# Two transformer blocks, fp32 products in three passes: another way to form the low part of the weights of the last product

## The reference, cut to what matters

```python
D_MODEL, SEQ, D_FF = 1024, 512, 2816

def second_block(x, ..., w_gate, w_up, w_down, final_norm_g):
    ...
    h = rmsnorm_2(x, ffn_norm_g[l])
    x = x + (jax.nn.silu(h @ w_gate[l]) * (h @ w_up[l])) @ w_down[l]
    return rmsnorm_2(x, final_norm_g)
```

## Time and profile before

| what | value |
|---|---|
| median of three timed executions | 1211.48 us |
| lowest and highest of them | 1210.47 and 1211.53 us |
| span of the profiled execution | 1209.1 us |
| TensorE busy, mean granted clock | 98% of the span, 0.998 of full speed |
| ScalarE busy, GpSimd busy | 46%, 41% |
| DMA traffic | 119.71 MB, all of it issued by SP, apart from instruction fetches |

### The profile page before, as it was taken

How to read it: one execution, slowest core, us unless ns; L and a number is a source line. 1 busy time by engine, 2 the same in 40 slices (tenths; PEclk the granted TensorE clock), 3 DMA queues, 4 the chain that set the end, 5 groups by cost and what they waited for, 6 DMA issues and landing times.

```text
span 1209.1 us, 15625 instructions
## 1 busy us (share of the span) xinstructions
PE 1188.8 (98%) x5810; PEld 990.9 (82%) x5810; DVE 629.7 (52%) x1459; ACT 561.4 (46%) x1009; POOL 499.3 (41%) x277
## 2 busy tenths in 40 slices
PE   9999999999999999999999999999999999999997
PEld 8878778888888887799878788788888888888886
DVE  5789864774628264999964773954222231220002
ACT  6453574476522364557765785434322332221114
POOL 1428462345433424123252883444344434443441
PEclk9999999999999999999999999999999999999999
DMA  8204662302332523153123204322332333323211
GB/s 276 81 25 142 173 175 70 105 1 71 122 105 70 186 94 105 35 176 108 36 40 94 81 23 153 103 93 84 105 105 70 105 105 103 102 74 122 104 70 70
DMA packets 80618, 119.71 MB, mean 99 GB/s; under 512 B 16024, under 2 KB 42776, under 8 KB 80160
## 3 DMA queue, kind: packets, MB, share of 16 engines
q1 hardware_dynamic: 80544, 118.71, 30.3%
HBM read 108.20 MB, written 4.21 MB: 93 GB/s over the span
## 4 chain that ended last, share of the span: by engine, by line
PE 80%; DVE 11%; ACT 2%; POOL 2%; issue 2%; DMA 2%; SPq 1%; DVEq 0%; ACTq 0%; POOLq 0%
PE bank L1794 59%; PE bank L2112 9%; PE bank L1858 2%; PE bank L1890 2%; PE bank L1872 2%; PE bank L1936 2%; DVE sc L1472 2%; DVE m L1468 1%; DVE sqS L1618 1%; POOL w_lo L731 1%; PE bank L1834 1%; DMA rot<-in_rot 1%; PE bank L1975 1%; DVE rp L1218 1%; ACT w_hi L834 0%
## 5 line engine op out<-in xcount | busy, mean ns | idle before, releaser
L714 POOL TENSOR_TENSOR w_lo<-w_raw,w_hi 128x2048 fp32r<-128x2048 f32 (+3 forms) x78 | 352.0, 4513 | 584.9 <-ACT w_hi L802 527.6
L1794 PE MATMUL bank<-aH,w_hi 128*128 128x512 f32 x832 | 331.6, 399 | 2.6 <-DVE mqT L1669 1.1
L1794 PE MATMUL bank<-aH,w_lo 128*128 128x512 f32 x832 | 324.9, 391 | 0.0
L1794 PE MATMUL bank<-aL,w_hi 128*128 128x512 f32 x832 | 318.2, 391 | 0.0
L802 ACT ACTIVATE w_hi<-w_raw 128x2048 fp32r<-128x2048 f32 (+3 forms) x74 | 138.4, 1870 | 262.1 <-PE bank L1794 159.5
L1794 PEld LDWEIGHTS bank<-aH,w_hi 128*128 128x128 f32 x832 | 157.0, 189 | 33.5 <-issue 4.7
L1794 PEld LDWEIGHTS bank<-aL,w_hi 128*128 128x128 f32 x832 | 156.3, 188 | 33.4
L1794 PEld LDWEIGHTS bank<-aH,w_lo 128*128 128x128 f32 x832 | 156.9, 189 | 27.8 <-issue 0.2
L1218 DVE TENSOR_TENSOR fg<-bank,rB 128x512 f32<-128x512 f32 x22 | 15.1, 691 | 128.2 <-PE bank L1794 128.2
L1794 PE MATMUL bank<-uH,w_hi 128*128 128x512 f32 x192 | 75.0, 391 | 0.3 <-DVE uL L1690 0.2
L1794 PE MATMUL bank<-uL,w_hi 128*128 128x512 f32 x192 | 74.8, 390 | 0.0
(11 more groups left out here) (337 smaller groups left out, 2124.2 us busy)
## 6 DMA issues: line engine op xcount, KB each, us to landing
w_raw<-in_w_in SPq DMA_DIRECT2D x21, 1024.0 KB, 5.0
w_raw<-in_w_gate SPq DMA_DIRECT2D x22, 512.0 KB, 3.9
w_raw<-in_w_up SPq DMA_DIRECT2D x22, 512.0 KB, 4.8
w_raw<-in_w_down SPq DMA_DIRECT2D x11, 1024.0 KB, 4.8
w_raw<-in_w_merge SPq DMA_DIRECT2D x8, 1024.0 KB, 4.9
w_raw<-in_w_out SPq DMA_DIRECT2D x8, 1024.0 KB, 4.9
w_raw<-in_w_ple_gate SPq DMA_DIRECT2D x4, 1024.0 KB, 4.9
w_raw<-in_w_in SPq DMA_DIRECT2D x4, 512.0 KB, 7.2
```

The costliest lines, as they stand in the source:

```text
L714: pool.tensor_tensor(out=w_lo[:, c % 2, 0:n], in0=w_raw[:, c % 2, 0:n], in1=w_hi[:, c % 2, 0:n].bitcast(F32), op=ALU.subtract).then_inc(w_ ...
L1794: ins = pe.matmul(o, l, r, start=(kk == 0 and operand == ROUNDED and m == 0), stop=(kk == total - 1 and operand == REST), skip_group_check ...
```

## The change

For the chunks of the unit `down`, GpSimd's subtraction is left out. ScalarE, after the hi part, waits for its own result and writes -hi into `w_lo` with a second activation (scale -1.0). GpSimd waits for that and issues a DMA from `w_raw` to `w_lo` in SBUF with `accum_op=add`, so that `w_lo` becomes raw - hi. TensorE, and SP before it reuses the raw buffer, wait for that DMA's semaphore `down_lo`. GpSimd waits before each of these DMAs until the one before has landed. All other chunks are made as before.

```diff
+        turned_ready, down_lo = sem("turned_ready"), sem("down_lo")
...
+        d_first = UNITS["down"][0]
+
+        def lo_wait(eng, c):
+
+            if c < d_first:
+                eng.wait_ge(w_lo_ready, c + 1)
+            else:
+                eng.wait_ge(down_lo, 16 * (c - d_first + 1))
...
                 if c >= 2:
                     sp_.wait_ge(w_hi_ready, c - 1)
-                    sp_.wait_ge(w_lo_ready, c - 1)
+                    lo_wait(sp_, c - 2)
...
             scale_rows("mla", sc2)
-            lo_through(len(CHUNKS) - 1)
+            lo_through(d_first - 1)
+            for c in range(d_first, len(CHUNKS)):
+                n = CHUNKS[c][0] * CHUNKS[c][1]
+                pool.wait_ge(turned_ready, c - d_first + 1)
+                if c > d_first:
+                    pool.wait_ge(down_lo, 16 * (c - d_first))
+                pool.dma_start(w_lo[:, c % 2, 0:n], w_raw[:, c % 2, 0:n], accum_op=ALU.add).then_inc(down_lo, 16)
...
                     act.activation(w_hi[:, c % 2, 0:n], w_raw[:, c % 2, 0:n], ACT.Copy).then_inc(w_hi_ready, 1)
+                    if c >= d_first:
+                        act.wait_ge(w_hi_ready, c + 1)
+                        act.activation(w_lo[:, c % 2, 0:n], w_hi[:, c % 2, 0:n].bitcast(F32), ACT.Copy,
+                                       scale=-1.0).then_inc(turned_ready, 1)
                     nxt[0] = c + 1
...
                 pe.wait_ge(w_hi_ready, c + 1)
-                pe.wait_ge(w_lo_ready, c + 1)
+                lo_wait(pe, c)
                 wh, wl = w_view(w_hi, c), w_view(w_lo, c)
```

## The result

The changed kernel takes 1214.67 us (median of 7 runs) against 1210.47 us of the kernel before on the same chip (7 runs); the ratio is 1.0032, interval 1.0020 to 1.0043. It is slower by 4.2 us by the two medians and by 3.9 us by the ratio; the prediction had 6.5 us, the right way and the right place, and too much.

The account below looks back on a forecast made before the run. TensorE was taken to bound the kernel. The terms 0 (GpSimd) + 0 (ScalarE's queue) + 6.5 us (DMA waits, 5 x 1.3) on 1211.5 us gave 1218.0 us, range 1210.6 to 1235.

Parts of the forecast that it names:

- The bound and the place: Last product: TensorE never waits and sets the pace; taking away GpSimd's subtraction gives nothing.
- Once per pair: Last product: TensorE waits at d2, d4, d6, d8 and d10 only, so each pair of chunks pays once, 5 x s.
- A: Adding DMA's time from GpSimd's release to its last semaphore: taken as 8.0 us, 8.25 with overlap; up to 6.95 fits.
- the longest of the 2 MB rows: Profiled 2 MB transfers took 7.3, 7.8 and 8.0 us; the 8.0 was taken for A as nearest in bytes read.
- My third way: Estimate of the adding DMA: a 1 MB load's 4.8 us plus 3.0 us for a second stream, 7.8 us.
- The budget: Each chunk's hi and lo must be ready 10.88 us after its buffer's release; 3.93 us before the DMA leaves it 6.95.
- The rival "no change": The DMA fits, A up to 7.4 us and loss below 2.4 us, time 1211.5 us; chance 0.3.
- the likeliest case: A between 7.4 and 10 us, losing 2.4 to 15 us, 1214 to 1227 us; chance 0.42.
- ScalarE's queue: Eleven added activations, 21.8 us, mostly in ScalarE's idle time; a Silu starts 0.5 us late; cost on the path 0.
- SP's queue: Loads of chunk c+2 start 5.3 us later but still land before ScalarE wants them, d4's at 1111 against 1117.
- The 0.25 us for the overlap with loads: Added to A where a load's end meets the next adding DMA; estimate 0.25 us, from 0 to 1.

Follow-up runs that it names:

- e2: Kernel before, with GpSimd's subtraction of each chunk of the last product done twice and no DMA of GpSimd's; 1214.42 us, ratio 1.0031.
- e4: Changed kernel with ScalarE's second activation done twice, the second time after a wait for the first; 1223.63 us, ratio 1.0104.
- e5: As e4, but only for d0, d2, d4, d6, d8, d10; the other chunks use GpSimd's subtraction as in the kernel before; 1226.34 us, ratio 1.0128.
- e7: Changed kernel with GpSimd's DMA as a plain copy instead of an addition, hi part's subtraction left out; 1210.19 us, ratio 0.9996.
- e6: Changed kernel with the load of gfin moved from behind the load of d4 to behind that of d10; 1214.46 us, ratio 1.0034.
- e8: Changed kernel with the second activation and the adding DMA each cut in two halves of 128x1024; 1228.06 us, ratio 1.0150.
- e9: As e8, with 1024 instead of 512 bytes per partition set aside for descriptors of GpSimd's DMAs; 1219.83 us, ratio 1.0078.

## Why the prediction came out as it did

**The bound and the place.** Right: TensorE sets the pace, GpSimd's subtraction was worth nothing to it, and the loss lies in the last product alone.

**Once per pair.** Right in kind (e2, e4, e5), not in its detail. I had waits at d2, d4, ... only, with releases 10.9 and 12.2 apart. But the DMAs' landings scatter (6.8 to 7.8 us). d3's took 7.8 us and moved the wait to the odd chunks d3 and d5, d6's took 7.3 and brought it back to the even ones. By the releases the time lost is 0.67 us at d2, 1.0 at d3, nothing at d4, 0.7 and 0.5 at d5 and d6, and 0.2 to 0.5 at each of the others.

**The duration of the DMA.** This is the term that was mis-sized. I took A = 8.25 us from ScalarE's end to the landing; it is 0.35 + 6.9 = 7.25 us. Of the reasons behind 8.25, the longest of the 2 MB rows was no good neighbour: that transfer comes from HBM, and e7 shows that a copy inside SBUF lands 0.3 us sooner than a load. My third way, one MB of load plus 3.0 us for the second stream, had too dear a stream: it costs 2.4 us.
The Trainium skill's page "DMA: Bandwidth & Descriptors" (section "Anatomy of one DMA") came nearest: its fit of 2.0 us plus bytes / 436 GB/s gives, as an estimate, 4.4 us for the copy and 6.8 for two streams; measured are 4.5 and 6.9. The Trainium skill's page "Collectives: The Full Stack" (section "The bandwidth ceiling") says of the adding step of a ReduceScatter that the addition costs nothing and its two reads halve the rate; 6.9 - 4.5 = 2.4 us is what a second MB costs by that fit. The trace agrees in the total, but 0.35 us of the 2.4 lie in GpSimd's longer issue.

**The budget.** The other error went the other way. I let the lo part land 10.88 us after the release; the cycle of a buffer has 0.43 to 0.49 us more in it, from the landing until TensorE runs at its pace. With both terms right, and counted from the hi part's start, it is 3.87 + 0.35 + 6.9 + 10.88 + 0.43 = 22.43 against 21.76, 0.67 us per pair and 3.4 us in all. With the landings that the trace has for each chunk in place of 6.9 (d3's 7.8, d6's 7.3) the same reckoning gives 4.0 us, against the 4.23 us of the trace. The two errors, 1.0 too much and 0.45 too little per pair, left 6.5 us in place of 4.

**The rival "no change".** It was nearer than its 0.3 says. I counted A from ScalarE's end, so the measured A is 7.25 us; by my own sum this costs 5 x 0.3 = 1.5 us, and I had put every A up to 7.4 under "no change". The loss is clear of no change only by the 0.45 us per pair that my budget left out. That the likeliest case came true is so in part luck: a DMA taken too long stood in for a budget taken too wide.

**ScalarE's queue, SP's queue.** Right. The first Silu behind d0's second activation starts late by less than 0.4 us and nothing follows from it; the loads land before they are wanted. The 0.25 us for the overlap with loads was not borne out as such: see e6.

## What to carry to other kernels

With two buffers the time from release to readiness may be one chunk's compute, less the half microsecond in which the consumer already wants its first operands; a preparation chain that exceeds it costs once per two chunks, whichever and however many of the two buffers' chains are slow. Before replacing an engine's step by a slower one, look for an order in which it needn't wait for its neighbour: here -round(raw) can be had from the raw words, and one swapped pair of activations makes the whole loss vanish. And a change that unloads an engine which nobody waits for, and whose work slows nobody, can at best end level.

## What the runs showed of the hardware

- An adding DMA of 1 MB within SBUF lands 6.9 us after its issue by GpSimd, a plain one after 4.5; it holds the DMA engines at a share of 0.95 while it writes 197 GB/s.
- With 512 bytes per partition for descriptors, GpSimd's next adding DMA of 128 rows (0.5 MB) wasn't issued until the one before had landed, even though GpSimd and the program were free (11 of 11; 5 of 11 with 1024, 2 of 11 with 1536).
- In e5 TensorE stopped five times, for 2.4, 2.4, 2.6, 2.3 and 2.4 us; behind the second and the fifth stop the granted clock fell to half for about 3 us, behind the others, the longest among them, it stayed full. It fell behind a stop of 3.1 us in e8 and did not behind one of 2.8 us in e9; what decides, these runs don't show. The windows of e9's stop and of the work behind it:

```profile
1116.30:1119.00 2.70, 0.00 (x0) 0.03 (x1) 0.00 (x0) 2.67 (x2) 0.00 (x0) 1.00 0.81 159
1119.00:1121.00 2.00, 2.00 (x9) 1.66 (x10) 0.00 (x0) 1.22 (x2) 0.87 (x1) 1.00 0.43 78
1121.00:1123.00 2.00, 2.00 (x11) 1.64 (x10) 0.00 (x0) 0.00 (x0) 0.00 (x0) 1.00 1.03 330
```
